# Delta heads: the chunk inverse applied once, to values less keys times state, with the dense blocks spread anew

## The reference, cut to what matters

```python
kb = k * beta[..., None]
Lmat = jnp.where(strict, jnp.einsum('bhnid,bhnjd->bhnij', kb, k) * decay, 0.0)
rhs = jnp.concatenate([v * beta[..., None], kb * jnp.exp(gc)[..., None]], axis=-1)
sol = lax.linalg.triangular_solve(eye + Lmat, rhs, left_side=True, lower=True, unit_diagonal=True)
value, k_cumdecay = sol[..., :DV], sol[..., DV:]
...
def step(state, xs):
    a_c, qd, kd, val, kcd, gl = xs
    v_new = val - jnp.einsum('bhcd,bhde->bhce', kcd, state)
    o = jnp.einsum('bhcd,bhde->bhce', qd, state) + jnp.einsum('bhij,bhje->bhie', a_c, v_new)
    state = state * gl[..., None, None] + jnp.einsum('bhcd,bhce->bhde', kd, v_new)
    return state, o
```

## Time and profile before

| | us |
|---|---|
| median of 3 runs | 1900.12 |
| lowest and highest of them | 1899.88, 1904.29 |
| the profiled execution's own time | 1897.6 |
| its span | 1895.5 |
| TensorE busy | 1867.9 (99%) |
| VectorE busy | 1210.9 (64%) |
| ScalarE busy | 788.7 (42%) |
| the delta stage, from the first L709 to the end of the last head | about 660 to 980 of the span |

### The profile page before, as it was taken

How to read it: one execution, slowest core, us unless ns; L and a number is a source line. 1 busy time by engine, 2 the same in 40 slices (tenths; PEclk the granted TensorE clock), 3 DMA queues, 4 the chain that set the end, 5 groups by cost and what they waited for, 6 DMA issues and landing times.

```text
span 1895.5 us, 29611 instructions
## 1 busy us (share of the span) xinstructions
PE 1867.9 (99%) x10550; PEld 1522.6 (80%) x10550; DVE 1210.9 (64%) x1877; ACT 788.7 (42%) x1481; POOL 301.3 (16%) x222
## 2 busy tenths in 40 slices
PE   9999999999999999999999999999999999999997
PEld 8888878888888767777778888888877888888886
DVE  7997554333333877777846846747778568476474
ACT  5234343233233555555534423424547444243242
POOL 0542232111011200001011100101222211011012
PEclk9999999999999999999999999999999999999999
DMA  5233323232222112111113332322411223322231
GB/s 210 89 100 100 134 72 107 90 106 93 100 89 100 45 57 71 56 60 62 51 57 100 100 111 77 103 97 89 134 67 45 73 84 111 100 93 96 89 107 71
DMA packets 46945, 170.47 MB, mean 90 GB/s; under 512 B 5344, under 2 KB 5504, under 8 KB 46720
## 3 DMA queue, kind: packets, MB, share of 16 engines
q1 hardware_dynamic: 45648, 165.12, 26.1%
q10 hardware_dynamic: 1200, 3.95, 0.6%
HBM read 166.94 MB, written 2.11 MB: 89 GB/s over the span
## 4 chain that ended last, share of the span: by engine, by line
PE 89%; DVE 6%; ACT 2%; issue 1%; POOL 0%; DVEq 0%; POOLq 0%; ACTq 0%
PE ps L276 19%; PE ps L278 18%; PE ps L277 18%; PE ps L264 9%; PE ps L266 9%; PE ps L265 9%; PE ps L732 1%; PE ps L757 1%; PE ps L709 1%; DVE scr L1579 1%; DVE scr L1570 1%; DVE Y L1570 1%; ACT Y L1502 0%; PE ps L802 0%; PE ps L741 0%
## 5 line engine op out<-in xcount | busy, mean ns | idle before, releaser
L223 ACT ACTIVATE w_hi<-w_raw 128x1024 fp32r<-128x1024 f32 x302 | 314.9, 1051 | 261.5 <-PE ps L278 172.0
L228 DVE TENSOR_TENSOR w_lo<-w_raw,w_hi 128x1024 fp32r<-128x1024 f32 x253 | 344.6, 1365 | 122.8 <-ACT w_hi L223 122.1
L276 PE MATMUL ps<-A_hi,w_hi 128*128 128x512 f32 x896 | 365.6, 408 | 1.3 <-DVE Y L1069 1.1
L278 PE MATMUL ps<-A_hi,w_lo 128*128 128x512 f32 x896 | 350.5, 391 | 0.0
L277 PE MATMUL ps<-A_lo,w_hi 128*128 128x512 f32 x896 | 349.6, 390 | 0.0
L276 PE MATMUL ps<-B_hi,w_hi 128*128 128x512 f32 x688 | 271.0, 394 | 1.3 <-DVE B_lo L1106 0.9
L278 PE MATMUL ps<-B_hi,w_lo 128*128 128x512 f32 x688 | 268.0, 389 | 0.0
L277 PE MATMUL ps<-B_lo,w_hi 128*128 128x512 f32 x688 | 267.8, 389 | 0.0
L276 PEld LDWEIGHTS ps<-A_hi,w_hi 128*128 128x128 f32 x896 | 168.3, 188 | 37.8 <-DVE Y L1069 2.5
L278 PEld LDWEIGHTS ps<-A_hi,w_lo 128*128 128x128 f32 x896 | 168.5, 188 | 36.1
L277 PEld LDWEIGHTS ps<-A_lo,w_hi 128*128 128x128 f32 x896 | 168.8, 188 | 29.2
(11 more groups left out here) (295 smaller groups left out, 2587.1 us busy)
## 6 DMA issues: line engine op xcount, KB each, us to landing
w_raw<-d_ws SPq DMA_DIRECT2D x304, 512.0 KB, 3.4
X<-d_xT SPq DMA_DIRECT2D x4, 512.0 KB, 7.1
X<-d_xT ACTq DMA_DIRECT2D x1, 2048.0 KB, 8.4
d_out<-X SPq DMA_DIRECT2D x4, 512.0 KB, 2.6
scr<-gc_rows ACTq DMA_DIRECT2D x7, 256.0 KB, 3.1
cst<-d_cst SPq DMA_DIRECT2D x1, 800.0 KB, 11.8
par<-d_par SPq DMA_DIRECT2D x1, 344.5 KB, 3.0
scr<-d_pw SPq DMA_DIRECT2D x1, 256.0 KB, 13.1
```

The costliest lines, as they stand in the source:

```text
L223: nc.scalar.activation(w_hi[:, c], raw[:, c], ACT.Copy).then_inc(S(f"w_hi{s}"), 1)
L228: nc.vector.tensor_tensor(w_lo[:, c], raw[:, c], w_hi[:, c].bitcast(F32), ALU.subtract)\
L276: pe.matmul(ps[bank][:], w_hi[:, c], hi, start=k == 0, stop=False)
L278: last = pe.matmul(ps[bank][:], w_lo[:, c], hi, start=False, stop=k == total - 1)
```

## The change

- KG, L789, WT and its copies go. For chunks 1 to 3 TensorE multiplies the keys, unscaled, by the state (into bank 5), VectorE makes that times exp(gc) less the scaled values, in place in VR, TensorE multiplies it by the inverse, and VectorE writes VN with the sign turned. The intra-chunk product L810 of a chunk now stands behind the next chunk's keys times state.
- Dense work is counted in single products. Ahead of the first level stand five blocks instead of six (three instead of four in head 0). In the recurrence a block stands behind each inverse product, one behind each state product (three of them) and, except in head 0, a single dense product behind each `keys times state` group: 8 blocks instead of 4 (7 instead of 4 in head 0). Behind it stand 1, 4 and 2 blocks instead of 2, 4 and 4 (0, 1, 1 instead of 0, 2, 2 in head 0).
- On VectorE, the taps of k move one chunk around, the product that ends q goes behind the last VN, and one of the two last half splits goes behind L1095.
- The Gram products write banks 3 and 2 instead of 4 and 3, and the wait for the squares (d_sq) goes from ahead of them to behind the five blocks.

```diff
-            pe.wait_ge(S("d_sq"), at("d_sq", 2 * NCH))
             for c in range(NCH):
-                last = pe.matmul(ps[4 - c // 2][:, (c % 2) * 256:(c % 2 + 1) * 256], KQv[:, c, 0, :],
+                last = pe.matmul(ps[3 - c // 2][:, (c % 2) * 256:(c % 2 + 1) * 256], KQv[:, c, 0, :],
                                  KQ[:, c * 256:(c + 1) * 256], start=True, stop=True)
...
-            dense(6, 4)
+            dense(5, 3)
             pe.wait_ge(S("zeros"), count("zeros", ZEROS))
+            pe.wait_ge(S("d_sq"), at("d_sq", 2 * NCH))
...
-            for i in range(2):
-                pe.wait_ge(S("d_tt"), at("d_tt", 13 + i))
-                if i == 0:
-                    pe.matmul(chunk(ps[3], 0), tt_of(0), chunk(VR, 0), start=True, stop=True).then_inc(S("d_pv"), 1)
-                for c in (2 * i, 2 * i + 1):
-                    last = pe.matmul(chunk(ps[4 + i], c % 2), chunk(KG, c), tt_of(c), start=True, stop=True)
-                last.then_inc(S("d_pw"), 1)
             for c in range(NCH):
-                val = ps[3 + 4 * (c % 2)][:, 0:P]
+                if c % 2 == 0:
+                    pe.wait_ge(S("d_tt"), at("d_tt", 13 + c // 2))
                 if c:
-                    pe.wait_ge(S("d_wt"), at("d_wt", c // 2 + 1))
                     pe.wait_ge(S("d_s"), at("d_s", c))
-                    pe.matmul(val, chunk(WT, c), ST[c % 2], start=False, stop=True).then_inc(S("d_pv"), 1)
+                    pe.matmul(ps[5][:, 0:P], KQv[:, c, 0, :], ST[c % 2], start=True, stop=True).then_inc(S("d_ks"), 1)
+                    pe.matmul(chunk(ps[6], c - 1), LAv[:, c - 1, 1, :], VN[(c - 1) % 2], start=c == 1, stop=True)
                     pe.matmul(chunk(ps[6], c), chunk(QD, c), ST[c % 2], start=True, stop=False)
-                if c < NCH - 1:
-                    pe.matmul(ps[3 + 4 * ((c + 1) % 2)][:, 0:P], tt_of(c + 1), chunk(VR, c + 1), start=True, stop=False)
+                    records(1 if h else 0)
+                    pe.wait_ge(S("d_sub"), at("d_sub", c))
+                pe.matmul(ps[3 + 4 * (c % 2)][:, 0:P], tt_of(c), chunk(VR, c), start=True, stop=True)\
+                    .then_inc(S("d_pv"), 1)
+                records(3)
                 pe.wait_ge(S("d_vn"), at("d_vn", c + 1))
                 if c < NCH - 1:
                     pe.matmul(ps[2][:, (c % 2 + 1) * P:(c % 2 + 2) * P], chunk(KD, c), VN[c % 2],
                               start=True, stop=True).then_inc(S("d_ps"), 1)
-                if more:
-                    dense(1)
...
-                last = pe.matmul(chunk(ps[6], c), LAv[:, c, 1, :], VN[c % 2], start=c == 0, stop=True)
-            last.then_inc(S("d_po"), 1)
+                    records(3)
+            pe.matmul(chunk(ps[6], NCH - 1), LAv[:, NCH - 1, 1, :], VN[(NCH - 1) % 2], start=False, stop=True)\
+                .then_inc(S("d_po"), 1)
+            dense(1, 0)
             if more:
-                dense(2, 0)
                 token_major_kq(pe, head_count(h + 1))
-                dense(4, 2)
...
+            dense(4, 1)
             pe.wait_ge(S("d_o1"), at("d_o1", NCH))
...
-            if more:
-                dense(4, 2)
...
+            dense(2, 1)
```

On VectorE:

```diff
             for c in range(NCH):
+                val = ps[3 + 4 * (c % 2)][:, 0:P]
+                if c:
+                    dve.wait_ge(S("d_ks"), at("d_ks", c))
+                    v.scalar_tensor_tensor(out=chunk(VR, c), in0=ps[5][:, 0:P], scalar=head_col(EGC, h, c),
+                                           in1=chunk(VR, c), op0=ALU.mult, op1=ALU.subtract).then_inc(S("d_sub"), 1)
                 dve.wait_ge(S("d_pv"), at("d_pv", c + 1))
-                v.tensor_copy(VN[c % 2], ps[3 + 4 * (c % 2)][:, 0:P]).then_inc(S("d_vn"), 1)
+                if c:
+                    v.tensor_scalar(VN[c % 2], val, -1.0, None, ALU.mult).then_inc(S("d_vn"), 1)
+                else:
+                    v.tensor_copy(VN[0], val).then_inc(S("d_vn"), 1)
                 if c < NCH - 1:
+                    conv(1, c + 1)
                     dve.wait_ge(S("d_ps"), at("d_ps", c + 1))
...
-                if c == 0:
-                    conv(1, 1)
-                elif c == 1:
+                else:
                     dve.wait_ge(S("d_la"), at("d_la", 5))
                     conv(0, 4)
-                elif c == 2:
-                    conv(1, 2)
-                else:
-                    conv(1, 3)
+            conv(1, 4)
             split(3, 0)
-            conv(1, 4)
-            split(3, 1)
             conv(2, 0)
...
+            split(3, 1)
             conv(2, 1, 2, 3)
```

More of the change, by code:

```diff
@@ L668, in delta_pe @@
             r = rnd(U_DELTA, h + 1)
[L670 to L690, removed]
-                    last.then_inc(S(f"unit_done{s}"), 1)
-            at_block = 0 if h else KT
-            def dense(n, n_first=None):
[L696 to L702, removed]
+            def record(s, k, j):
+                if k == 0 and j == 0:
+                    if more:
+                        unit_wait(pe, r, s)
+                    else:
+                        pe.wait_ge(S(f"w_hi{s}"), count(f"w_hi{s}", rnd(U_AOUT, 0) + 1))
+                        pe.wait_ge(S(f"w_lo{s}"), count(f"w_lo{s}", rnd(U_AOUT, 0) + 1))
+                        if s < 2:
+                            pe.wait_ge(S(f"evac{s + 2}"), count(f"evac{s + 2}", rnd(U_AOUT, 0)))
+                if not more and j == 0:
+                    o_wait(pe)(k)
+                pair = pairA if more else pairB
+                c = slice(s * 1024 + k * P, s * 1024 + (k + 1) * P)
+                last = pe.matmul(ps[s % 2 if more else open_bank(s, 4)][:], (w_hi, w_hi, w_lo)[j][:, c],
+                                 tile(pair[j % 2], k), start=k == 0 and j == 0, stop=k == KT - 1 and j == 2)
+                if k == KT - 1 and j == 2:
+                    last.then_inc(S(f"unit_done{s}"), 1)
@@ new lines, in delta_pe, with records @@
+            at_record = 0 if h else 3 * KT
+            end_record = 3 * (4 if more else 2) * KT
+            def records(n):
+                nonlocal at_record
+                for _ in range(n):
+                    s, k, j = at_record // (3 * KT), at_record // 3 % KT, at_record % 3
+                    if at_record < end_record and (more or k < KT - 1):
+                        record(s, k, j)
+                    at_record += 1
+            def dense(n, n_first=None):
+                records(3 * (n if h or n_first is None else n_first))
@@ L783, in delta_pe @@
                 fill(l, 1)
[L784 to L790 removed]
+            if not more:
+                at_record, end_record = end_record, 2 * end_record
             for c in range(NCH):
[L792 removed]
+                if c % 2 == 0:
+                    pe.wait_ge(S("d_tt"), at("d_tt", 13 + c // 2))
                 if c:
[L794 removed]
                     pe.wait_ge(S("d_s"), at("d_s", c))
[L796 removed]
+                    pe.matmul(ps[5][:, 0:P], KQv[:, c, 0, :], ST[c % 2], start=True, stop=True).then_inc(S("d_ks"), 1)
+                    pe.matmul(chunk(ps[6], c - 1), LAv[:, c - 1, 1, :], VN[(c - 1) % 2], start=c == 1, stop=True)
                     pe.matmul(chunk(ps[6], c), chunk(QD, c), ST[c % 2], start=True, stop=False)
[L798 to L799 removed]
+                    records(1 if h else 0)
[3 more added lines that the diff above has]
+                records(3)
                 pe.wait_ge(S("d_vn"), at("d_vn", c + 1))
@@ L920, in delta_act @@
                         conv_tanh(act, h + 1, 0)
-            for i in range(2):
-                act.wait_ge(S("d_pw"), at("d_pw", i + 1))
-                a.activation(WT[:, 2 * i * P:2 * (i + 1) * P], ps[4 + i][:, 0:2 * P], ACT.Copy, scale=-1.0)\
-                    .then_inc(S("d_wt"), 1)
             if more:
@@ L931, in delta_act @@
             act.wait_ge(S("d_orow"), at("d_orow", 1))
+            act.wait_ge(S("d_ro"), at("d_ro", 0))
             token_scale(act, "d_o1", KG, 6, lambda c: TK[:, 28 + c:29 + c])
```

24 lines of the change are left out of this document (7 added, 17 removed).

## The result

The changed kernel takes 1908.25 us (median of 5 runs, 1907.87 to 1910.77) against 1900.12; the ratio is 1.0042 [1.003, 1.0053]. It is **slower**, by 0.42%, just outside the range.

The account below looks back on a forecast made before the run. TensorE is full, partly with filler, and VectorE's chain ends last behind the recurrence. Per full head +1.69 - 1.71 = 0.0, or +0.2; in sum 0 to +1.2 us on 1897.6, forecast 1900.9 (no change), range 1892 to 1908.

Parts of the forecast that it names:

- Part 3: Last VN to first level: VectorE ends last, so the stretch gets only 1.71 us shorter and TensorE waits.
- Part 2: Recurrence, first inverse product to last VN: all hops covered, 0.04 to 0.14 us to spare; 1.69 us longer, 8.62.
- the rival of the uncovered hops: Five covers per head: a missed one costs 0.2 us, 1.0 per head; kernel 1904 to 1908, slower; chance 0.2.
- a moved step said to be hidden: After the last VN: the moved half split fits VectorE's idle wait for ScalarE's tap; 0.6 us if not.
- The clock: TensorE's new waits of 1.2 and 0.4 us in every head cost no clock: no loss taken.
- The rival that every head's wait at L732 costs the clock: L732 of every head: the clock falls, 1.6 us each by head 0's price; kernel 1910, slower; chance 0.1.
- The sum: Whole kernel: six full heads 0 to 1.2 us, head 0 +0.9, last head -0.9; together 0 to +1.2 us.

Follow-up runs that it names:

- the second experiment: The changed kernel with both half splits of the last gap moved behind the state updates of chunks 1 and 2: 1901.83 us, ratio 1.0016.
- the fourth experiment: The changed kernel with idle products, 12 and 9 of 128 columns, ahead of head 0's two long waits: 1907.78 us, ratio 1.0047.
- the best version: The changed kernel with half splits and the product ending q moved, key squares early on ScalarE, idle products in head 0: 1896.99 us, ratio 0.9988.

## Why the prediction was wrong

**What held.** VectorE bounds the stretch ahead of the levels: L732 was to wait 1.2 us and L757 0.4, they wait 1.09 and 0.21. That the first wait came out so close is partly luck: both engines reached L732 later than added up, VectorE's part 0.4 and TensorE's 0.5 us. VN to L1080 was right within 0.01, L757 to the first inverse product is unchanged (15.39, 15.38 before), and chunk 0 took 1.84 for 1.83. TensorE was relieved of its products and none of it reached the end, as Part 3 said.

**The step that failed: Part 2, the price of a hop.** "With an operation of 0.35 like L1077 it is 0.83", and the covers were to fit "with 0.04 to 0.14 us to spare". I took the start delay of the plain copy (0.42) for both forms. The operation with a scalar per row starts 0.53 after its product, so its hop is 0.93; its cover is 0.90. Two of the three hops of a chunk are of this form. What it costs is more than the 0.02 to 0.03 by which it misses: a product that had to wait lasts 0.49 instead of 0.38 and passes 0.12 on. Chunk 1 grows by 0.03 at the first hop, 0.12 from the inverse's product to the state's and 0.12 from there to the next keys' product (1.03 each for 0.91); what remains of the recurrence likewise, in all 0.75: 9.37 for 8.62. The run without the scalar gives 0.42 of it back (shown). The state's update was not tried in another form; its part rests on the rows, where it starts 0.53 behind L801. The rows of before had it: L802 at 767.34 to L1077 at 767.97 is 0.63, 0.1 of a product that had waited and 0.53 of the form, and I read only the copy's 0.42 off them. This is the rival of the uncovered hops, "a missed one costs 0.1 of wait and 0.1 to restart", which I gave 0.2.

**Part 3, a moved step said to be hidden.** The half split behind L1080 fits VectorE's idle time, but runs beside GpSimd's power, which takes 1.39 us instead of 1.01, and VectorE gets this back through ScalarE: 12.57 for 12.34. Shown by the second experiment, where it is 12.25. This term had the right place and the wrong sort of cover: I looked at the engine it runs on, not at its neighbour. The Trainium skill (SBUF — State Buffer, "Who interferes with whom") says that a VectorE instruction with two SBUF inputs contends with a GpSimd instruction that reads SBUF, and the later one stands still. The trace agrees: the split (two tiles, from 781.78) is 0.69 long, the power starts 0.17 behind it at 781.95 and is 0.38 longer in heads 0 to 6.

**The clock: "I take no loss".** In head 0 the wait at L732 grew from 2.05 to 2.88 and that of the output transposes from 1.06 to 2.12; granted clock 0.92 instead of 0.96, and head 1's Gram product took 3.57 us for 1.99. Kept busy, head 0 falls by 2.9 us. Part of the forecast's own reasoning was at fault: it used head 0's clock for the price of a rival and not for head 0 itself, where its waits were to grow. The price was too high as well: 1.6 us stood, the idle products gave the kernel before 0.94 in head 0, and the fall in head 4 of the fourth experiment cost 1.4. For heads 2 to 6 no loss was right, but not safe: the fourth experiment shows heads 1 and 4 at the lower level after waits of 1.30 and 1.13 us, and heads 2, 3, 5 and 6 at full clock after waits of 1.10 to 1.12. The rival that every head's wait at L732 costs the clock is refuted by these; that none does is refuted too.

**The sum.** Counted as the prediction counts, each head up to the L757 of the next: head 0 +3.7 us (52.26 for 48.53) where +0.9 stood. With the idle products in both kernels it is 49.37 for 47.59, +1.78, near the 0.9 with the 0.75 and 0.23 of the two steps above; the other 1.95 is what the lower clock costs more than before. Then heads 1 to 6 together +5.7 (243.14 for 237.42) where 0 to 1.2 stood, 0.75 and 0.23 a head as above; the last head -0.4 where -0.9 stood: its recurrence 9.27 for 9.06, its levels +0.5 for +0.4, and its output transposes 0.1 earlier (4.24 us behind L804 for 4.36) where up to 0.3 stood, as they wait for ScalarE's scaling by 0.30. These make 9.1 of the 10.5 us.

**What stays open.** Why the same waits cost the clock in some heads and not in others. What the state's update would cost in another form. And whether the best version's 1.1 us over the eight heads can be seen in the kernel's time: its ratio and that of the kernel before with idle products, 0.9988 and 0.9987, are the same within their intervals.

## What to carry to other kernels

Price a hop by the form of the instruction that makes it, start delay included, and add the restart of the product behind it: a cover that misses by 0.03 costs 0.12. Work taken off a full engine is won only if the next chain is shorter too; add up that chain first, and move its work into the gaps that the change itself has made longer (the same moves cost the kernel before 0.4%). Where an order is written by hand, the number of fillers ahead of a point fixes which evacuations stand ready behind it; one fewer cost 20 us here.

## What the runs showed of the hardware

- VectorE's 128x128 operation from PSUM starts 0.42 us after its product as a copy or a subtraction of two tensors, 0.53 as a scalar_tensor_tensor with a scalar per row (772.10 against 771.57), though it is itself only 0.06 longer (0.35 and 0.29).
- A float32 product behind a hop that isn't covered lasts 0.46 to 0.49 instead of 0.38. Where it is late by some hundredths, as in the changed kernel, no idle time is reported ahead of it and the loss is seen only in its duration and in the next start.
- GpSimd's 128x4 power takes 1.39 us instead of 1.01 when a 128x512 subtraction of two SBUF tiles runs on VectorE at its start, in each of heads 0 to 6.
- TensorE's clock can fall to its lower level after waits of 1.13 + 0.21 us (head 4 of the fourth experiment, 0.96) and stay at 1.00 after 1.11 + 0.21 in the next head, and after 1.13 + 0.20 in head 5 of the changed kernel.
